# Tile 3 of each norm: its last slabs in column halves, mean and variance from statistics instructions

## What is computed

```python
for layer in range(DEPTH):                      # DEPTH = 2
    h = conv_sgu_mixer(x, ...) if layer % 2 == 0 else dilated_attention_mixer(x, ...)
    x = layer_norm(DN_ALPHA * x + h, ln_g[layer, 0], ln_b[layer, 0])
    x = layer_norm(DN_ALPHA * x + swiglu(x, w_gate, w_up, w_down), ln_g[layer, 1], ln_b[layer, 1])
# layer_norm: mu = mean(x); var = mean((x - mu)**2); (x - mu) * rsqrt(var + eps) * g + b
```

## Time and profile before

| | |
|---|---|
| median of 3 runs | 1435.24 us (1434.02 to 1435.37) |
| the profiled execution | 1433.95 us |
| its span, first to last instruction | 1432.2 us |
| TensorE busy | 1397.7 us, 98% of the span |
| VectorE / ScalarE / GpSimd busy | 504.7 (35%) / 492.0 (34%) / 634.3 (44%) us |
| mean granted clock of TensorE | 0.995 of full speed |
| chain that ended last | TensorE 85%, VectorE 8%, GpSimd 3%, ScalarE 2% |

### The profile page before, as it was taken

The page is one execution under the profiler, slowest core; times in us unless marked ns, Lnnn a source line. Parts: engine busy times, 40 slices in busy tenths (PEclk is TensorE's granted clock), DMA queues, the critical chain, the costliest instruction groups (busy, mean ns, idle before and its releaser), DMA issues.

```text
span 1432.2 us, 17148 instructions
## 1 busy us (share of the span) xinstructions
PE 1397.7 (98%) x6695; PEld 1186.8 (83%) x6695; DVE 504.7 (35%) x702; ACT 492.0 (34%) x742; POOL 634.3 (44%) x295
## 2 busy tenths in 40 slices
PE   7998999999999998999999999999999999999997
PEld 6876888888888888888898888899888888888886
DVE  4987511111140035666532665732141111110003
ACT  4464532232321243333322333333253222232213
POOL 5875454444444444333432332433244444444443
PEclk9999999999999999999999999999999999999998
DMA  9222233333432323233322322332123333342321
GB/s 280 80 88 72 76 104 95 96 98 92 134 100 92 103 59 100 63 88 88 104 88 74 88 73 75 86 121 88 45 68 110 88 103 97 94 131 92 101 74 59
DMA packets 175326, 134.75 MB, mean 94 GB/s; under 512 B 4213, under 2 KB 157577, under 8 KB 175272
## 3 DMA queue, kind: packets, MB, share of 16 engines
q1 hardware_dynamic: 175272, 133.98, 31.0%
HBM read 131.87 MB, written 2.10 MB: 94 GB/s over the span
## 4 chain that ended last, share of the span: by engine, by line
PE 85%; DVE 8%; POOL 3%; ACT 2%; issue 2%; DMA 0%; DVEq 0%; SPq 0%; ACTq 0%; POOLq 0%
PE pq L571 17%; PE pq L573 17%; PE pq L572 17%; PE pq L595 6%; PE pq L593 6%; PE pq L594 6%; DVE pq L1357 3%; PE pq L890 3%; PE pq L891 3%; PE pq L892 3%; POOL x_res L505 1%; POOL w_lo L497 1%; PE pq L868 1%; PE pq L828 1%; PE pq L841 1%
## 5 line engine op out<-in xcount | busy, mean ns | idle before, releaser
L497 POOL TENSOR_TENSOR w_lo<-w_stage,w_hi 128x1024 fp32r<-128x1024 f32 x236 | 568.5, 2414 | 750.8 <-ACT w_hi L980 750.7
L571 PE MATMUL pq<-xt_hi,w_hi 128*128 128x512 f32 (+1 forms) x1272 | 480.3, 378 | 1.2 <-POOL w_lo L497 1.1
L572 PE MATMUL pq<-xt_lo,w_hi 128*128 128x512 f32 (+1 forms) x1272 | 476.6, 375 | 0.0
L573 PE MATMUL pq<-xt_hi,w_lo 128*128 128x512 f32 (+1 forms) x1272 | 476.4, 375 | 0.0
L980 ACT ACTIVATE w_hi<-w_stage 128x1024 fp32r<-128x1024 f32 x236 | 246.0, 1054 | 254.7 <-PE pq L595 183.8
L571 PEld LDWEIGHTS pq<-xt_hi,w_hi 128*128 128x128 f32 x1272 | 239.8, 189 | 45.5 <-DVE xt_lo L1273 1.8
L573 PEld LDWEIGHTS pq<-xt_hi,w_lo 128*128 128x128 f32 x1272 | 239.6, 188 | 43.2
L572 PEld LDWEIGHTS pq<-xt_lo,w_hi 128*128 128x128 f32 x1272 | 239.8, 189 | 42.0
L1519 DVE TENSOR_TENSOR hidden<-pq,hidden 128x512 f32<-128x512 f32 x44 | 30.4, 692 | 367.8 <-PE pq L573 367.8
L593 PE MATMUL pq<-w_hi,ht_hi 128*128 128x512 f32 x352 | 137.1, 390 | 0.0
L595 PE MATMUL pq<-w_hi,ht_lo 128*128 128x512 f32 x352 | 137.0, 389 | 0.0
(11 more groups left out here) (185 smaller groups left out, 1335.9 us busy)
## 6 DMA issues: line engine op xcount, KB each, us to landing
w_stage<-in_od_w_qkv_dram SPq DMA_DIRECT2D x72, 512.0 KB, 3.8
w_stage<-in_ffn_w_gate_dram SPq DMA_DIRECT2D x44, 512.0 KB, 3.8
w_stage<-in_ffn_w_up_dram SPq DMA_DIRECT2D x44, 512.0 KB, 3.8
w_stage<-in_ffn_w_down_dram SPq DMA_DIRECT2D x44, 512.0 KB, 3.4
w_stage<-in_ev_w_in_dram SPq DMA_DIRECT2D x16, 512.0 KB, 6.4
w_stage<-in_ev_w_out_dram SPq DMA_DIRECT2D x8, 512.0 KB, 3.4
w_stage<-in_od_w_out_dram SPq DMA_DIRECT2D x8, 512.0 KB, 3.5
x_res<-in_x_dram SPq DMA_DIRECT2D x4, 512.0 KB, 6.1
```

What stands on the lines that cost most here:

```text
L497: pool.tensor_tensor(w_lo[slab % RING][:, :], w_stage[slab % RING][:, :], w_hi[slab % RING][:, :].bitcast(F32), ALU.subtract).then_inc(w_l ...
L571: pe.matmul(ps[bank][:, at], hi[:, k, :], xt_hi[:, k, at], start=(k == 0), stop=False)
L572: pe.matmul(ps[bank][:, at], hi[:, k, :], xt_lo[:, k, at], start=False, stop=False)
L573: last = pe.matmul(ps[bank][:, at], lo[:, k, :], xt_hi[:, k, at], start=False, stop=(k == KD - 1))
```

## The change

For token tile 3 alone, at each of the four norms. TensorE multiplies the last three slabs into half 0 of the columns first (nine matmuls, then `acc_half`), turns tile 0 of the next product, multiplies slab j = 0 into half 1, turns tile 1, and multiplies slabs 1 and 2 into half 1. VectorE adds alpha * x half by half, without a row sum, and takes the mean and variance from `bn_stats` on each half and one `bn_aggr`; half 0 is done ahead of `low(0)` and `norm_gain(e, 2)`. ScalarE's Square of tile 3 is gone; it takes the root of the variance. `norm_gain` of tile 3 waits for the mean alone. The root's wait and the counts of `acc_done` and `ln_sq` follow (three a norm).

```diff
@@ finish_tiles (TensorE)
-                for i in range(TILES):
+                for i in range(SHIFT_TILES):
                     for j in range(3):
                         last = both_halves(slab + j, t_hi, t_lo, row + j, i, False, j == 2)
-                        if i == TILES - 1:
+                    last.then_inc(acc_done, 1)
+                i = SHIFT_TILES
+                for half in range(2):
+                    for j in range(3):
+                        last = tokens(slab + j, 512 * half, 512, pq[:, 2 * i + half, :], t_hi[:, row + j, :],
+                                      t_lo[:, row + j, :], i, False, j == 2)
+                        if half:
                             last.then_inc(w_used, 1)
-                            if j < 2 and e < 3:
-                                turn_x(e + 1, j)
-                    if i < TILES - 1:
-                        last.then_inc(acc_done, 1)
+                            if j == 0 and e < 3:
+                                turn_x(e + 1, 1)
+                    if half == 0:
+                        last.then_inc(acc_half, 1)
+                        if e < 3:
+                            turn_x(e + 1, 0)
@@ root (ScalarE)
+                    if i == SHIFT_TILES:
+                        act.activation(std[:, i:i + 1], mean_var[:, i, 1:2], ACT.Sqrt, bias=eps[:, 0:1]
+                                       ).then_inc(ln_std, 1)
+                        return
@@ new (VectorE)
+            def norm_half(e, half):
+
+                i = SHIFT_TILES
+                if half == 0:
+                    dve.wait_ge(acc_half, e + 1)
+                else:
+                    dve.wait_ge(w_used, (S_UP0, S_ATT, S_UP1, N_SLABS)[e])
+                bank = pq[:, 2 * i + half, :]
+                link.mark(dve.scalar_tensor_tensor(out=bank, in0=x_res[:, i, half * 512:(half + 1) * 512], scalar=ALPHA,
+                                                   in1=bank, op0=ALU.mult, op1=ALU.add))
+                link.wait()
+                link.mark(dve.bn_stats(stats[:, 6 * half:6 * half + 6], bank))
+                if half:
+                    link.wait()
+                    link.mark(dve.bn_aggr(mean_var[:, i, :], stats[:, :]))
+                    link.wait()
+                    dve.tensor_scalar(neg_mean[:, i:i + 1], mean_var[:, i, 0:1], -1.0, None, ALU.mult
+                                      ).then_inc(row_summed, 1)
@@ norm_gain (VectorE)
-                dve.wait_ge(ln_sq, e * TILES + i + 1)
+                if i < SHIFT_TILES:
+                    dve.wait_ge(ln_sq, e * SHIFT_TILES + i + 1)
+                else:
+                    dve.wait_ge(row_summed, e * TILES + i + 1)
@@ norm, the order (VectorE)
                 norm_in(e, 2)
+                norm_half(e, 0)
                 low(0)
                 low(1)
                 norm_gain(e, 2)
                 norm_scale(e, 2)
-                norm_in(e, 3)
+                norm_half(e, 1)
                 norm_gain(e, 3)
```

More of the change, by code:

```diff
@@ L233, in trunk @@
         acc_done = sem("acc_done")
+        acc_half = sem("acc_half")
         ln_std = sem("ln_std")
@@ L998, in root @@
                                    ).then_inc(ln_sq, 1)
-                    act.wait_ge(ln_sq, n + 1)
+                    act.wait_ge(ln_sq, e * SHIFT_TILES + i + 1)
                     act.activation(std[:, i:i + 1], sq_sum[:, i:i + 1], ACT.Sqrt, bias=eps[:, 0:1],
@@ L1277, in norm_in @@
             def norm_in(e, i):
[L1279 to L1282, removed]
+                dve.wait_ge(acc_done, e * SHIFT_TILES + i + 1)
                 banks = tile_banks(i)
```

## The result

The changed kernel takes 1436.93 us (median of 20 runs, 1435.03 to 1440.61), the kernel before 1434.66 (20 runs, 1433.64 to 1436.17). The ratio is 1.0016, with a 95% interval of 1.0010 to 1.0022: slower by 2.3 us, between 1.4 and 3.2, which is under the 2.9 us (0.2%) that the prediction took as the line of "no change". The forecast was slower by 2.07 us, a median of 1437.3, and "no change" as the likeliest verdict.

A forecast was written before the change was run, and what follows sets the result against it. TensorE, busy 98% of the span, was taken as the bound, with a store stream ending the tail. Norms 1.74 plus tail 0.33 gave +2.07 us, a median of 1437.3, range 1434.7 less a bit of run spread to 1439.1.

The forecast's parts named there:

- The late turn: Three norms: tile 0's turn 0.68 us later delays ScalarE and VectorE, 0.58 us a norm, +1.74 us in all.
- VectorE's cover: Three norms: VectorE's idle 0.70 and 1.10 us take in the added half addition and statistics, cost 0.
- Rival 3: VectorE's queue: PSUM statistics at twice the price (1.33 us), tail costs 1.0, +2.7 us in all, 1438.0; chance 0.08.
- The tail: Fourth norm: last half written 0.54 us sooner, but tile 2's later store delays the full DMA stream, +0.33 us.
- Rival 4: Norms: TensorE's new idle gap lowers the granted clock; one norm dropping adds 1.7 us, 3.8 in all, 1439.0; chance 0.06.
- the sum: Whole kernel: 1.74 us for three norms plus 0.33 for the tail, 2.07 us slower.

The follow-up runs named there:

- e1: Kernel before with only the turn of tile 0 issued nine of tile 3's matmuls in, not six; ratio 1.0017, median 1436.54 against 1433.73 us.
- e7: Kernel before with the turn of tile 0 twelve of tile 3's matmuls in, not six; ratio 1.0016, median 1437.27 against 1434.79 us.
- e6: Changed kernel, norms 0 to 2: turn back behind six matmuls, VectorE's halves behind tile 2's root; fourth norm as before; ratio 1.0005.
- e2: Changed kernel with the turn of tile 0 back behind six of tile 3's matmuls, all vector operations kept; ratio 1.0015, median 1436.95 against 1433.73 us.
- e4: Kernel before with the change at the fourth norm alone; ratio 1.0003 (0.9994 to 1.0012).
- e9: Kernel before with halves and statistics at the fourth norm only, plus tile 2's rows stored in two column halves; ratio 0.9999, median 1435.36 against 1434.84 us.
- e10: Kernel before with only tile 2's final store split into two column halves; ratio 0.9996, median 1434.02 against 1434.84 us.
- e8: Changed kernel run again without an edit, against the kernel before; ratio 1.0012, median 1435.93 against 1434.79 us.
- e11: Kernel before, unedited, profiled a second time; tail 9.61 us from the last matmul's start to the end of the span.
- e12: Kernel before, unedited, profiled a third time; tail 9.42 us from the last matmul's start to the end of the span.
- e3: Kernel before with the change at norms 0, 1 and 2 only, fourth norm as before; ratio 1.0008, median 1435.32 against 1433.73 us.
- e5: Changed kernel plus three unused matmuls at norms 0 to 2 in the gap ahead of the first slab; ratio 1.0011, median 1435.9 against 1434.79 us.

## Why the prediction was right, and where it was not

**The late turn: right, size and place.** 0.58 us a norm was worked out; the profiles have 0.54, 0.48 and 0.56 at the first slab and about the same at the turn of tile 2. The chain after is the one that was described. The first turn is 0.68 later (10.01 against 9.32 from the norm's first addition), ScalarE's pair takes 1.06 in place of 1.31, and VectorE's pair 1.29 in place of 1.42, as in the working. The idle time ahead of the first slab is 0.60, not 0.76. e1 shows that the order on TensorE alone does it, e7 that three more matmuls pass on one for one (0.69 for 0.68), e6 that with the turn back and the halves behind nothing is lost.

**VectorE's cover: right for this kernel.** Half addition 0.70 and statistics from PSUM 0.70 (estimates: 0.67 each), with 0.84 us idle left. (By the prediction's own numbers `low(0)` is 0.3 late, not 0.2: 1055.71 against 1055.41. It changes nothing.) What the prediction did not say is how thin the order is: e2, where the half addition starts 0.9 us later, loses 0.5 us by VectorE's queue alone. Rival 3 needed a dear instruction; a late start does the same.

**The tail: right in the sum, by pooled profiles.** Tile 2's gain is 0.38 later (worked out 0.33), the last half 0.48 sooner (0.54), and the end 0.3 later over twelve profiles (0.33). In the one profile of after the tail is 0.06 shorter than in the one of before; single tails of one kernel differ by up to 0.44 (9.86 and 9.42), so this could be read only from several. That the stream of transfers sets the end fits e4, where the last half is sooner and the end is not, and the transfers of e9; in e10 the stream has a gap, and there the last half holds the end.

**The clock: the step that failed.** Rival 4 had the granted clock fall only where TensorE idles as the 1.97 us of the earlier trace rows did, "none is that long", and a chance of 0.06; the sum put the clock at nothing. In the profile of after it fell in the second and the third norm, behind idle times of 1.10 and 0.57 us. The third norm (the turns behind the first of these waits, then stretches with TensorE's busy time, granted clock, DMA share, GB/s):

```profile
1069.09 0.66 PE L608 MATMUL pq<-ident,x_res 128*128 128x128 f32 x4 [1.10 <-POOL x_res L506]
...
1069.00:1071.00 2.00, 1.34 (x9) 0.93 0.81 245
1071.00:1073.00 2.00, 2.00 (x11) 0.50 0.06 17
1073.00:1075.00 2.00, 2.00 (x15) 0.71 0.00 0
```

The next stage is 1.0 us late in the second norm (39.10 against the 38.11 of e1 and e8) and 1.6 in the third (35.15 against 33.55). With the 1.6 us of the path these make 4.2 of the 4.9 us that the profiled execution is longer. Most of the rest lies ahead of the first norm, which begins 0.9 later (154.63 against 153.75): there too the clock is low in a stretch in which it is full before (0.50 from 118.5 to 125.2).

Nor does a longer idle time always bring the clock down. Behind the second norm TensorE waits 2.26 us in both kernels. In the profile of before the clock then falls, in e11, the same kernel, it doesn't (row and stretch of before, then of e11):

```profile
564.71 0.80 PE L831 MATMUL pq<-qk 128*128 128x128 f32 x2 [2.26 <-DVE qk L1568]
...
564.70:568.00 3.30, 3.29 (x9) 0.50 0.53 157
```

```profile
565.62 0.49 PE L831 MATMUL pq<-qk 128*128 128x128 f32 x2 [2.26 <-DVE qk L1568]
...
565.60:569.10 3.50, 3.48 (x17) 1.00 0.51 148
```

So the length of the idle time alone, on which the rival rested, does not decide it. Over the fourteen profiles the clock fell in 3 of the 21 norms with the order of before, all three in the first norm of the kernel (e6, e9, e12), and in 5 of the 21 with a late path (after, e3, e5), all in the second or third. The prediction looked at one profile of before, in which no norm had it, and took that for the kernel's state.

**How much of the hit is luck.** The forecast started from 1435.24, a median of three runs; twenty runs gave 1434.66. The absolute forecast is 0.4 us high and the difference 0.2 low. And the measured difference of 2.3 holds executions with the lower clock on both sides, which the sum left out. The 1.6 us of the path are no luck; that the whole agrees to 0.2 us is in part luck.

**What stays open.** The path and the tail give 1.6 + 0.3 = 1.9 us, and the medians differ by 2.3 (1.4 to 3.2) in the first comparison and the runs by 1.1 to 1.7 in e8. But e7's runs are only 2.3 to 2.5 us longer where its norms lose 3.6. The mean granted clock of each execution, which is on record, accounts for much of this. The kernel before ran 87 times beside the experiments, in three sets; in 47 of them the mean clock is 0.994 or less, and in each set these are 1.8 to 2.1 us longer in the median than the others. Of the 33 executions of e5, e7 and e8 none is under 0.995, against 18 of 33 of before in the same set. Against the other 15 of before (median 1433.67) e7 is 3.6 us longer (3.3 by the means), what its norms lose, and e8 2.3 (2.5). On this reading the plain comparison there hides a part of the price of the late turn behind the lower clock that before has in half of its executions. The opposite is on record too: 6 of the 20 executions of the changed kernel in the first comparison have 0.991 or 0.992, and they are its six slowest (1438.67 and more); none of the 87 of before is under 0.993. It is therefore not shown that the change leaves the clock alone: how often and where it falls differs between the kernels. The split is coarse (e6's profile has a fall in a norm at 0.995), and in the set of e1 and e2 it leaves 3.1 and 3.4 us where the profiles give 1.6 and 1.8. Why the clock falls in one execution and not in another with the same idle times stays open.

## What to carry to other kernels

Before work of another tile is put ahead of a transpose, follow who waits for the transpose through every queue in written order: three matmuls (0.68 us) ahead of it cost 0.5 us a norm, with the same number of instructions on TensorE, because ScalarE's and VectorE's queues had no gap behind them. Finishing sooner what nobody waits for (tile 3 in three norms; the last half ahead of a full transfer stream) returns nothing. And where the granted clock can fall in single stretches of 3.4 us, compare kernels by the distances between two rows in several profiles, and look whether a fall lies between them: without one, kernels with the same path agreed here to 0.1 us, where the times of one kernel's runs differ by up to 4 us. The mean granted clock of every run then tells how often such falls come in each kernel.

## What the runs showed of the hardware

- Statistics over 128x512 from PSUM take 0.70 us (from SBUF 0.67); an addition of 128x512 with one operand in PSUM 0.67 to 0.70, its form with 1024 columns 1.21; an aggregate of two groups 0.21, of one 0.18.
- The granted clock of TensorE differs between executions of one kernel at the same place: 1.00 in one (e11), 0.50 for 3.3 us in another (e12), behind the same idle times of 1.10 and 0.57 us; and behind an idle time of 2.26 us it was 0.50 in one (before) and 1.00 in another (e11). Each such fall from the 2.4 to the 1.2 GHz level costs 1.0 to 1.6 us in these norms. It came with the idle time of 0.6 us ahead of the first slab filled with matmuls (e5), and did not come in the one profile with an idle time of 1.28 us there (e7).
- Three stores of 512, 256 and 256 KB in a row move at 369 and 372 GB/s. With the first of them issued 0.36 us later and the data of the last ready 0.48 sooner, the kernel ends 0.3 us later (means of five and seven profiles).
